# VectorE makes the modulation tiles from the weight ring; ScalarE's conv activations stand one projection later

## The reference, cut to what matters

```python
c_act = silu(c)
for i in range(2):
    mod = c_act @ w_mod[i] + b_mod[i]          # 1024 x 6144 weights a layer
    shift_m, scale_m, gate_m, shift_f, scale_f, gate_f = split(mod, 6)
    h = rms_norm(x, norm_mix_pre[i]) * (1 + scale_m) + shift_m
    y = hybrid_mixer(h, ...)                   # h @ w_in; attention, SSD scan, short conv; @ w_out
    x = x + gate_m * rms_norm(y, norm_mix_post[i])
    h = rms_norm(x, norm_ffn_pre[i]) * (1 + scale_f) + shift_f
    y = swiglu(h, w1, w3, w2) if i == 0 else moe_swiglu(h, ...)
    x = x + gate_f * rms_norm(y, norm_ffn_post[i])
```

## Time and profile before

| | us |
|---|---|
| median of 3 runs | 1982.06 |
| lowest, highest | 1978.17, 1986.73 |
| the profiled execution, its time | 1986.19 |
| its span, first to last instruction | 1984.5 |

### The profile page before, as it was taken

The page is one execution under the profiler, slowest core; times in us unless marked ns, Lnnn a source line. Parts: engine busy times, 40 slices in busy tenths (PEclk is TensorE's granted clock), DMA queues, the critical chain, the costliest instruction groups (busy, mean ns, idle before and its releaser), DMA issues.

```text
span 1984.5 us, 24928 instructions
## 1 busy us (share of the span) xinstructions
PE 1767.4 (89%) x8953; PEld 1490.2 (75%) x8953; DVE 1433.2 (72%) x1114; ACT 1100.2 (55%) x971; POOL 538.3 (27%) x382
## 2 busy tenths in 40 slices
PE   5779779998686868689999999999999999999994
PEld 5768669887575866568788787888878888788883
DVE  5875756555575454378888888888888888889884
ACT  1444333333233333276767767777676777767772
POOL 1658517999665540101010010100101001010001
PEclk9789889999788879689999999999999999999997
DMA  9436545666444453379999999999999999999993
GB/s 307 149 117 212 181 148 175 219 234 216 142 150 149 145 185 126 108 256 380 363 363 382 353 380 359 364 376 359 380 358 369 371 359 385 355 370 367 363 383 136
DMA packets 290309, 550.29 MB, mean 277 GB/s; under 512 B 14006, under 2 KB 114632, under 8 KB 290248
## 3 DMA queue, kind: packets, MB, share of 16 engines
q1 hardware_dynamic: 281968, 533.76, 75.8%
q0 software_dynamic: 3888, 14.16, 2.1%
q10 hardware_dynamic: 4392, 1.57, 0.3%
HBM read 540.55 MB, written 8.91 MB: 277 GB/s over the span
## 4 chain that ended last, share of the span: by engine, by line
PE 53%; POOLq 19%; issue 16%; DVE 5%; DMA 3%; ACT 2%; POOL 1%; DVEq 1%; SPq 0%; ACTq 0%
PE ps L1510 17%; PE ps L1512 16%; PE ps L1511 16%; POOLq L707 7%; POOLq L709 6%; DVE lo_ring L1439 3%; POOLq L712 2%; POOLq L717 2%; POOLq L714 2%; DMA pool_mod<-in_w_mod_dram 2%; PE ps L1823 1%; ACT stage_hi L970 1%; DMA weight_ring<-in_w_mod_dram 1%; PE ps L1540 1%; POOL rstd L690 0%
## 5 line engine op out<-in xcount | busy, mean ns | idle before, releaser
L1439 DVE TENSOR_TENSOR lo_ring<-weight_ring,stage_hi 128x2048 fp32r<-128x2048 f32 x378 | 848.7, 2286 | 108.7 <-ACT stage_hi L970 108.3
L970 ACT CAST stage_hi<-weight_ring 128x2048 fp32r<-128x2048 f32 x378 | 704.1, 1913 | 97.5 <-DMA weight_ring<-in_moe_w_dram 89.8
L1510 PE MATMUL ps<-stage_hi,xe_hi 128*128 128x512 f32 x1008 | 407.1, 404 | 8.7 <-DVE lo_ring L1439 8.7
L1511 PE MATMUL ps<-lo_ring,xe_hi 128*128 128x512 f32 x1008 | 396.8, 394 | 0.0
L1512 PE MATMUL ps<-stage_hi,xe_lo 128*128 128x512 f32 x1008 | 396.2, 393 | 0.0
L1079 DVE TENSOR_TENSOR lo_ring<-weight_ring,stage_hi 128x2048 fp32r<-128x2048 f32 x81 | 213.9, 2642 | 188.2 <-ACT stage_hi L827 186.8
L1510 PE MATMUL ps<-h_hi,stage_hi 128*128 128x256 f32 x800 | 243.1, 304 | 48.0 <-ACT xbcT L817 35.4
L745 POOL TENSOR_TENSOR tick<-neghalf 128x1 f32<-128x1 f32 x9 | 18.7, 2078 | 925.1 <-DVE xidx L1403 925.1
L1511 PE MATMUL ps<-h_lo,stage_hi 128*128 128x256 f32 x800 | 236.8, 296 | 0.0
L1512 PE MATMUL ps<-h_hi,lo_ring 128*128 128x256 f32 x800 | 236.1, 295 | 0.0
L1510 PEld LDWEIGHTS ps<-stage_hi,xe_hi 128*128 128x128 f32 x1008 | 189.9, 188 | 54.4 <-DVE lo_ring L1439 13.4
(11 more groups left out here) (299 smaller groups left out, 2050.8 us busy)
## 6 DMA issues: line engine op xcount, KB each, us to landing
weight_ring<-in_moe_w_dram SPq DMA_DIRECT2D x378, 1024.0 KB, 5.2
pool_mod<-in_w_mod_dram SPq DMA_DIRECT2D x80, 512.0 KB, 3.8
weight_ring<-in_w_in_dram SPq DMA_DIRECT2D x36, 1024.0 KB, 6.6
weight_ring<-in_ffn_w_dram SPq DMA_DIRECT2D x33, 1024.0 KB, 6.5
weight_ring<-in_w_out_dram SPq DMA_DIRECT2D x12, 1024.0 KB, 8.3
weight_ring<-in_w_mod_dram SPq DMA_DIRECT2D x8, 1024.0 KB, 14.1
moe_rows<-y_e POOLq DMA_DIRECT2D x10, 512.0 KB, 8.2
moe_rows<-y_moe POOLq DMA_DIRECT2D x3, 512.0 KB, 3.9
```

Source lines behind the costliest of these rows:

```text
L970: nc.scalar.copy(jst_hi[i % JSTAGES][:], ring[:, n % RING, :]).then_inc(hi_ready, 1)
L1439: nc.vector.tensor_tensor(ring_lo[:, n % RING, :], ring[:, n % RING, :], raw(jst_hi[i % JSTAGES][:]), ALU.subtract).then_inc(lo_ready, 1)
L1510: mm(dst, lh, rh, start=start, stop=False)
L1511: mm(dst, lh, rl, start=False, stop=False)
```

## The change

All 40 tiles move from GpSimd and `pool_mod` to VectorE and the weight ring: they become "mod" steps, which stand at places written in `BEHIND`, in the new `WITHIN` (beside `w_out`) and by a rule in the channel mixer. `pool_mod`, its loads, its semaphores and GpSimd's passes over it are gone; GpSimd keeps the norm factors. TensorE's sum (now always "modcol") stands two steps behind its tile. The tiles are dealt out anew: 12, 19 and 9 in place of 12, 16 and 12, and the last four of the first mixer (`LATE`) go beside `w_out`, with a "modfin" of their own.

ScalarE's SiLU of a conv ("conv_out") is taken one step after VectorE's convolution, behind the next split. The copy of the short convolution ("sconv_split") and the attention norm's multiply ("attnorm") move back by a step as well. TensorE's transposes "ssdT" go from before the third `w_out` slot to before the fourth, and the first `w_out` slot takes its second token block first, so that it waits for the last copy of a projection only half way.

```diff
 BEHIND = {
-    0: [("dt_sp", 0), ("conv", 0)], 1: [("conv", 1)], 2: [("cum_sub", 0), ("conv", 2)], 3: [("conv", 3)],
+    0: [("dt_sp", 0), ("conv", 0)], 1: [("conv_out", 0), ("conv", 1)], 2: [("conv_out", 1), ("cum_sub", 0), ("conv", 2)],
+    3: [("conv_out", 2), ("conv", 3)], 4: [("conv_out", 3), ("tile", 0)],
...
-    8: [("pt_out", 1), ("pv_out", 0), ("exp", 2), ("pd", 2)],
+    8: [("pt_out", 1), ("pv_out", 0), ("exp", 2), ("pd", 2), ("tile", 2)],
...
+WITHIN = {0: [("tile", 8), ("ssdn", 0)], 1: [("tile", 9)], 2: [("tile", 10)], 3: [("tile", 11)]}
+TILES = {"mix0": [(0, i) for i in range(8, 20)],
+         "ffn": [(0, i) for i in range(20, 24)] + [(1, i) for i in range(15)],
+         "mix1": [(1, i) for i in range(15, 24)]}
+LATE = TILES["mix0"][8:]
+SUM_AT = [7, 9, 10, 11, 12, 13, 14, 15, 16]
+LATE_SUM_AT = [2, 3, 4, 4]
...
-            if n == 2:
+            if n == 3:
                 s.append(("ssdT", l, 0))
...
+                    if made < len(tiles) and done >= 5 * made // 3:
+                        s.append(("mod",) + tiles[made])
+                        made += 1
...
-                if stream[n][0] == "split":
-                    while n_pm < len(pool_tiles) and pool_at[n_pm] == stream[n][1]:
-                        l, i = pool_tiles[n_pm]
-                        for half in range(2):
-                            if n_pm:
-                                sp.wait_ge(pm_used, 2 * n_pm + half - 1)
-                            sp.dma_start(pm[:, half], k_rows(w_mod[l], half * KT // 2, KT // 2, i * 256, 256)
-                                         ).then_inc(pm_landed[half], 16)
...
-                        nc.gpsimd.tensor_tensor(w, w, cb, ALU.mult)
-                        nc.gpsimd.drain()
-                        nc.gpsimd.tensor_tensor(w[:, 0:2, :], w[:, 0:2, :], w[:, 2:4, :], ALU.add)
...
-                elif name == "conv":
+                elif name == "conv_out":
                     act.wait_ge(conv_acc, 4 * l + i + 1)
...
+                    if (l, i) in LATE:
+                        pe.wait_ge(mixl_ready, 4 * l + 3)
...
                     if i == 0:
-                        pe.wait_ge(proj_out, NOUT * (l + 1))
...
+                    for t, k in sorted(blocks_last(True), reverse=True) if i == 0 else blocks_last(i == 5):
+                        if i == 0 and (t, k) == (0, 1):
+                            pe.wait_ge(proj_out, NOUT * (l + 1))
```

More of the change, by code:

```diff
@@ L155, in schedule, with steps @@
         s.append(("norm", l, 0))
-        tiles = POOL_TILES["mix%d" % l]
-        s.extend(("pmod",) + one for one in tiles)
+        tiles = TILES["mix%d" % l]
+        def steps(names):
+            for name, j in names:
+                s.append(("mod",) + tiles[j] if name == "tile" else (name, l, j))
         for i in range(NOUT):
@@ L185, in schedule @@
         if l == 0:
-            tiles = POOL_TILES["ffn"]
-            s.extend(("pmod",) + one for one in tiles)
-            summed = 0
+            tiles = TILES["ffn"]
+            made = summed = 0
             for q in range(NQ + 1):
```

127 lines of the change are left out of this document (44 added, 83 removed).

## The result

| | before | after |
|---|---|---|
| median | 1981.76 us, 4 runs (1978.17 to 1986.73) | 1880.97 us, 4 runs (1878.8 to 1884.8) |
| span of the profiled execution | 1984.5 | 1879.9 |

The ratio is 0.949, with a 95% interval of 0.947 to 0.952: 101 us less, where the prediction had 105 less (1877, range 1850 to 1925). The stages show that the total hides errors that cancelled. They are cut at the same slots in both kernels; in layer 0 they begin at 52.5 us before and at 51.6 after. By the profiled executions, from which the table is made, they come to 105 us less, as predicted; the terms that were missed one way (both first steps, 16 us too little) and the other way (attention in layer 0, the channel mixer, the tails, attention in layer 1, 16 us too much) cancel.

A forecast was written before the change was run, and what follows sets the result against it. The prediction took GpSimd's tiles to set the channel mixer's time and to hold SyncE's queue in the mixers. Its stage terms, -27 - 22 - 17 + 7 - 20 - 11 - 13 - 2, made -105 us: 1877, range 1850 to 1925.

The forecast's parts named there:

- first steps: Steps 0 to 7 of each mixer: relieved convs and splits and a later SiLU gain 22 us and 17 us.
- attention in layer 0: Steps 8 to 15: late ring landings delay pd in three short steps, costing 7 us (0 to 20).
- the channel mixer: Stage of 232.6 us set by GpSimd: falls to 206, -27 us, with TensorE narrowly leading VectorE.
- the tails: From z to the last w_out slot: waits removed or hidden, -11 us in layer 0, -13 in layer 1.
- attention in layer 1: Steps 8 to 15: late ring transfers vanish without waits on GpSimd, 104.3 to 84 us, -20.
- the stretch: VectorE's instructions slowed beside GpSimd: 0.36 us back per split, up to 5.5 us per stretched conv.
- the second rival's sign: ScalarE waiting for ring landings in the channel mixer would show that the ring has too few places.
- VectorE becomes the bound: Rival, chance 0.14: VectorE's instructions stay stretched though GpSimd is idle, 44 us less gain, near 1921 us.
- The ring is too short: Rival, chance 0.15: ScalarE stands for landings in the channel mixer too, +26 and +15 us, near 1912 us.
- Every tile is exposed: Rival, chance 0.05: TensorE waits for the whole of each tile, 137 us more, 2014 us, slower than before.
- the tiles were not the bound: Rival, chance 0.06: the channel mixer's lost time mostly has another cause that stays, near 1969 us.
- The clock stays up: Rival, chance 0.10: each removed wait gives back more clock behind it, 15 to 25 us more gain, near 1857 us.

The follow-up runs named there:

- e7: The kernel before, with the loads of GpSimd's tiles issued by GpSimd itself instead of SyncE: 2083.9 us, ratio 1.050.
- e6: The kernel before, with GpSimd's passes over its tiles cut to eight columns, loads and waits kept: 1871.1 us, ratio 0.944.
- e2: The changed kernel with the conv's SiLU, the short convolution's copy and the attention norm's multiply put back: 1913.0 us, ratio 0.963.
- e9: The changed kernel with only the four SiLUs of the convolutions put back behind their own projection: 1908.0 us, ratio 0.960.
- e1: The changed kernel with seven places in the weight ring in place of six: 1858.9 us, ratio 0.936.
- e5: The changed kernel with only the first of eight passes made for the 40 tiles; whole not compared, channel mixer 202.7 us.
- e8: The changed kernel with seven ring places and layer 0's third late tile moved behind VectorE's part of ssdT: 1861.1 us, ratio 0.938.
- e3: The changed kernel with GpSimd doing passes on a scratch buffer that nobody waits for, for 36 tiles: 2025.3 us, ratio 1.020.

## Why the prediction came out as it did

**The mechanism was right.** GpSimd's passes set the channel mixer's time: slowed in e7 they lengthen it, taken out in e6 they leave 201.5 us. That their own pace does it is shown by the waits for tiles; what the stretch of VectorE added there is not. With the passes off and nothing else changed, the kernel takes 0.944 of before (e6). Making the tiles on VectorE from the ring, with the moves at w_out and without the other three, costs 0.020 of it (e2 less e6, 39 us); the three moves give back 0.014 (28 us). Each of these two is uncertain by some 5 to 7 us, since each ratio is by up to 0.0026. The prediction had this structure, but its sum was made stage by stage and did not show how much each cause weighs.

**The first steps were undersized, -22 and -17 against -30.3 and -24.6.** The failed term is the stretch. I relieved VectorE's 69.5 us by two or three convs' 5.5 and eight splits' 0.36, to "some 56" with a tile. It was 48.6 with a tile, and 46.4 without the tile in e6: 23 us of the 69.5 had been stretch. I had the split's mean over 81, while in this stretch a split took 2.73, a conv's first pass 1.02 in place of 0.41, a later one 0.75 in place of 0.48, and h_lo 1.06 in place of 0.69. The convs together gave back 11 us and the splits 4, close to what I had counted; the other 8 came from instructions that I had at nothing, h_lo and the small ones of dt above all (a `dtz` of 16 elements took 1.68 us before and 0.11 in e6). The tile, too, took 3.75 us of work, not 4.27. The remaining chain that I kept (dt's small instructions, "tok") did not hold TensorE: its only recorded wait in the stage is 3.4 us for h_lo. The cover by the SiLU's place was rightly seen; it is 10.4 us of the 30.3 (e9), the passes 19.4 (e6).

**Attention in layer 0, +12.9 against +7.** The step was right in kind and number: three waits for pd of up to 1.9 us where 2.4 was worked out, and ScalarE at a landing five times. The size was off for two reasons. I priced the waits and not the clock that follows them: 10.3 us at half clock are about 5 us of TensorE's work more. And I took the 76.6 us of before as what remains without GpSimd, while e6 shows 72.8, `lr` having cost 1.04 us a time beside it and 0.22 without. Of the 16.7 us above that, e1 gives 11.2 to the ring, e5 6.4 to the passes; the two overlap by a microsecond.

**Attention in layer 1, -18.9 against -20.** Right in the number, by two misses that offset each other: the stage would be 74.4 us without GpSimd's passes (e6), not the 76.6 that I built on, and tiles and ring cost 11.0 above it, not 7. The expected nearness to layer 0 was missed by a microsecond (4.1, not 3).

**The channel mixer, -22.4 against -27.** VectorE's load was wrong by 27 us (193 against 165.8, 79% busy and not over 85%). Of these 16 are again the stretch (27.7 us of the 124.1 by e6, 12 counted), and 10 are the gaps between a tile's passes, which I had counted as work (19 x 4.27 = 81 against 71.1). The stage still came out near, because TensorE leads it. Its 205 was too low by 5. Without the passes of the tiles it is 202.7 (e5), so 7.5 are theirs, of which 4.4 are recorded waits for sums. No such wait was over 1.2 us, as expected. ScalarE's waits for landings, the second rival's sign, were there too (19.9 us in 10 waits, the longest 3.4), but a seventh place brought only 2.7 us.

**The tails, -7.5 and -12.6 against -11 and -13.** z starts 0.7 us behind the slot before it, as expected. In layer 0, VectorE's part of ssdT stood behind the third late tile:

```profile
245.36 0.80 PE L1480 MATMUL ps<-stage_hi,h_hi 128*128 128x512 f32 x1 [7.28 <-DVE h_lo L1281]
```

I had looked at the tile ahead of the SSD norm and not at this one, one slot on. e8 and e5 show that taking that wait away wins a microsecond at most, so the miss of 3.5 us is not explained by it.

**The rivals.** "VectorE becomes the bound" fell with 2.29 us a split. "The ring is too short" was true where its sign was not looked for, and worth 22 us over all, by e1: 11.2 and 7.4 in the two attention stages, 3.4 in the norms ahead of the channel mixer, and 2.7 in the channel mixer, less what the tails lost. "Every tile is exposed" fell with the 4.4 us of waits for 19 tiles, and "the tiles were not the bound" with e6. "The clock stays up" was true in the first steps (0.80 to 0.91), and was paid back in layer 0's attention (0.98 to 0.90). e3 shows how the first rival would have looked.

## What to carry to other kernels

Where GpSimd and VectorE both work out of SBUF, take the contention from each instruction's own duration with and without GpSimd beside it, stage by stage: here a split of 2048 elements was stretched by a quarter and an `lr` of one element nearly fivefold, and a mean over the splits hides it. Work moved into a queue of fixed depth costs places, not only time; count how many steps ahead a transfer can still be issued, and look for the engine that stands for a landing, also in the stage behind (the norms here), and try one place more with the memory that the move frees. When a wait is taken away, name the next one in line before counting a gain.
